# Weight products of a four-layer network: the outputs of a product take turns matmul by matmul, instead of one output after the other

## The reference, cut to what matters

```python
x = x + forgetting_attention(rmsnorm(x), fox_w_in, ..., fox_w_out)   # proj = h @ w_in ... o @ w_out
x = x + swiglu(rmsnorm(x), w_in, w_out)      # gu = h @ w_in; (silu(gate) * up) @ w_out, D_FF = 2816
x = x + retention(rmsnorm(x), w_in, w_out)   # w_in is 1024 x 6144, w_out 2048 x 1024
x = x + swiglu(rmsnorm(x), w_in, w_out)
x = x + rmsnorm_2(nsa_mixer(rmsnorm_2(x), ...))
x = x + rmsnorm_2(diff_mixer(rmsnorm_2(x), ...))
```

## Time and profile before

| | |
|---|---|
| median of 3 runs | 2217.71 us (2216.29 to 2219.92) |
| the profiled execution | 2220.15 us |
| its span | 2218.8 us |
| mean granted TensorE clock | 0.987 of full speed |
| PE busy | 2133.1 us, 96% of the span |
| DVE / ACT / POOL busy | 1002.5 / 783.7 / 254.8 us |
| DMA | 190.47 MB, 86 GB/s |

### The profile page before, as it was taken

How to read it: one execution, slowest core, us unless ns; L and a number is a source line. 1 busy time by engine, 2 the same in 40 slices (tenths; PEclk the granted TensorE clock), 3 DMA queues, 4 the chain that set the end, 5 groups by cost and what they waited for, 6 DMA issues and landing times.

```text
span 2218.8 us, 26618 instructions
## 1 busy us (share of the span) xinstructions
PE 2133.1 (96%) x10149; PEld 1720.7 (78%) x10149; DVE 1002.5 (45%) x2026; ACT 783.7 (35%) x1485; POOL 254.8 (11%) x360
## 2 busy tenths in 40 slices
PE   6999999999999999999999999899989999899978
PEld 4887887888878875888888888677867778688657
DVE  4437524444354336355434433543355553522575
ACT  4326332222232223333322222333355553332472
POOL 0103000000002100000100000010035552000250
PEclk9999999999999999999999999999999999999999
DMA  4330232333324320322333332243210002333211
GB/s 158 105 95 11 76 117 86 96 95 95 95 96 122 97 86 19 95 95 67 124 95 99 100 95 86 83 146 100 78 62 34 34 34 95 100 98 99 77 39 48
DMA packets 96766, 190.47 MB, mean 86 GB/s; under 512 B 8407, under 2 KB 16639, under 8 KB 96512
## 3 DMA queue, kind: packets, MB, share of 16 engines
q1 hardware_dynamic: 90288, 164.35, 24.6%
q0 software_dynamic: 6352, 24.41, 3.3%
HBM read 184.48 MB, written 4.26 MB: 85 GB/s over the span
## 4 chain that ended last, share of the span: by engine, by line
PE 86%; DVE 7%; ACT 4%; issue 2%; POOL 1%; DMA 0%; ACTq 0%; DVEq 0%; SPq 0%; POOLq 0%
PE bank L671 64%; PE bank L704 7%; PE bank L1095 4%; PE bank L1065 2%; PE bank L1076 2%; PE bank L936 2%; DVE wl L1742 1%; ACT junk L1259 1%; PE bank L1066 1%; DVE hTl L1814 1%; DVE xn L1804 1%; PE bank L921 1%; PE bank L1006 1%; PE bank L740 1%; PE bank L1102 1%
## 5 line engine op out<-in xcount | busy, mean ns | idle before, releaser
L1742 DVE TENSOR_TENSOR wl<-raw,wh 128x1024 fp32r<-128x1024 f32 x306 | 376.2, 1234 | 833.3 <-ACT wh L1220 832.6
L1220 ACT ACTIVATE wh<-raw 128x1024 fp32r<-128x1024 f32 x306 | 320.9, 1053 | 899.4 <-PE bank L671 875.5
L671 PE MATMUL bank<-hTh,wh 128*128 128x512 f32 (+1 forms) x1328 | 517.4, 390 | 0.2 <-issue 0.2
L671 PE MATMUL bank<-hTl,wh 128*128 128x512 f32 (+1 forms) x1328 | 516.8, 389 | 0.0
L671 PE MATMUL bank<-hTh,wl 128*128 128x512 f32 (+1 forms) x1328 | 516.7, 389 | 0.0
L671 PEld LDWEIGHTS bank<-hTh,wh 128*128 128x128 f32 (+1 forms) x1328 | 248.0, 187 | 53.6 <-issue 0.3
L671 PEld LDWEIGHTS bank<-hTh,wl 128*128 128x128 f32 (+1 forms) x1328 | 248.0, 187 | 53.0
L671 PEld LDWEIGHTS bank<-hTl,wh 128*128 128x128 f32 (+1 forms) x1328 | 248.0, 187 | 53.0
L671 PE MATMUL bank<-wh,hTh 128*128 128x512 f32 x464 | 181.6, 391 | 1.2 <-DVE hTl L2442 1.1
L671 PE MATMUL bank<-wh,hTl 128*128 128x512 f32 x464 | 180.7, 389 | 0.0
L671 PE MATMUL bank<-wl,hTh 128*128 128x512 f32 x464 | 180.6, 389 | 0.0
(11 more groups left out here) (351 smaller groups left out, 2784.7 us busy)
## 6 DMA issues: line engine op xcount, KB each, us to landing
raw<-in_ffn_w_in SPq DMA_DIRECT2D x88, 512.0 KB, 3.6
raw<-in_ret_w_in SPq DMA_DIRECT2D x48, 512.0 KB, 3.8
raw<-in_ffn_w_out SPq DMA_DIRECT2D x44, 512.0 KB, 3.7
raw<-in_diff_w_in SPq DMA_DIRECT2D x32, 512.0 KB, 3.7
raw<-in_fox_w_in SPq DMA_DIRECT2D x24, 512.0 KB, 3.8
raw<-in_nsa_w_in SPq DMA_DIRECT2D x20, 512.0 KB, 3.6
raw<-in_ret_w_out SPq DMA_DIRECT2D x16, 512.0 KB, 3.7
bt<-bias_by_lag POOLq DMA_DIRECT2D x16, 448.0 KB, 3.9
```

Of the source, the lines that this page charges most:

```text
L671: i = pe.do.matmul(dst, x, y, start=first and k == 0 and q == 0, stop=stop)
L1220: act.do.activation(M.hl[n % HL_SLOTS][0][:, 0:m], M.raw[n % RAW_SLOTS][:, 0:m], ACT.Copy).then_inc(*T.up("act_hi", n))
L1742: dve.do.tensor_tensor(wl[:, 0:m], M.raw[n % RAW_SLOTS][:, 0:m], wh[:, 0:m].bitcast(F32), ALU.subtract).then_inc(*T.up("dve_lo", n))
```

## The change

In every chunk but a product's last, the loops run k, then q, then o: the three matmuls of a step are each issued for all outputs in turn, so that successive matmuls go to different banks. The wait for the activations of a step and an output stands before the first of its three matmuls, and the wait for the bank behind it, in the product's first step. In the last chunk the order is that of before. A product of one chunk is all last chunk.

```diff
-        for o in range(n_out):
-            b = banks[o]
-            if first:
-                pe_bank(pe, T, b)
-            pe_weights(pe, T, n)
-            for k in range(nk):
-                for name, key in ready(k0 + k, None if mode == "F" else o):
-                    pe.wait_ge(*T.at(name, key))
...
-                for q, (x, y) in enumerate(parts):
-                    stop = last and k == nk - 1 and q == 2
-                    done = k == nk - 1 and q == 2 and o == n_out - 1
-                    i = pe.do.matmul(dst, x, y, start=first and k == 0 and q == 0, stop=stop)
...
+        pe_weights(pe, T, n)
+        if last:
+            for o in range(n_out):
+                if first:
+                    pe_bank(pe, T, banks[o])
+                for k in range(nk):
+                    operands(k, o)
+                    for q in range(3):
+                        step(o, k, q)
+                pe.free[banks[o]] = freed(o)
+        else:
             for k in range(nk):
...
+                for q in range(3):
+                    for o in range(n_out):
+                        if q == 0:
+                            operands(k, o)
+                            if first and k == 0:
+                                pe_bank(pe, T, banks[o])
+                        step(o, k, q)
```

More of the change, by code:

```diff
@@ L651, in pe_product, with step @@
         first, last = k0 == 0, k0 + nk == rows
-        for o in range(n_out):
+        def step(o, k, q):
             b = banks[o]
-            if first:
-                pe_bank(pe, T, b)
-            pe_weights(pe, T, n)
-            for k in range(nk):
-                for name, key in ready(k0 + k, None if mode == "F" else o):
-                    pe.wait_ge(*T.at(name, key))
[L660 to L667, removed]
-                for q, (x, y) in enumerate(parts):
-                    stop = last and k == nk - 1 and q == 2
-                    done = k == nk - 1 and q == 2 and o == n_out - 1
-                    i = pe.do.matmul(dst, x, y, start=first and k == 0 and q == 0, stop=stop)
[L672 to L675, removed]
@@ new lines, in step @@
+            h, l = operand(k0 + k)
+            if mode == "F":
+                f1 = min(width, o * 128 + 128)
+                x, y = wh[:, k, o * 128:f1], wl[:, k, o * 128:f1]
+                dst, (x, y) = M.bank[b][0:f1 - o * 128, :], ((x, h), (x, l), (y, h))[q]
+            else:
+                cols = slice(o * 128, o * 128 + 128)
+                dst, (x, y) = M.bank[b][:, 0:width], ((h[:, cols], wh[:, k, :]), (h[:, cols], wl[:, k, :]), (l[:, cols], wh[:, k, :]))[q]
+            stop = last and k == nk - 1 and q == 2
@@ new lines, in step, with operands @@
+            done = k == nk - 1 and q == 2 and o == n_out - 1
+            i = pe.do.matmul(dst, x, y, start=first and k == 0 and q == 0, stop=stop)
+            if stop or done:
+                i.then_inc(*T.up("pe_product", *[(tag, o)] * stop, *[("chunk", n)] * done))
+        def operands(k, o):
+            for name, key in ready(k0 + k, None if mode == "F" else o):
+                pe.wait_ge(*T.at(name, key))
+        pe_weights(pe, T, n)
[8 more added lines that the diff above has]
+                pe.free[banks[o]] = freed(o)
+        else:
+            for k in range(nk):
+                for q in range(3):
[5 more added lines that the diff above has]
+                        step(o, k, q)
```

## The result

The changed kernel is slower: ratio 1.0053 to the kernel before, 95% interval 1.0033 to 1.0073. Its four runs have a median of 2231.82 us (2226.51, 2231.55, 2232.1, 2232.4), beside 2218.82 us for the kernel before. On the earlier median of 2217.71 us the ratio gives 2229.5 us; the median of the four itself lies 0.8 us above the range's upper end. The profiled execution is the fastest of the four: 2226.51 us, span 2225.2 us, granted clock 0.986. In the changed kernel the matmul of the products stands on L666 and not L671, and the lines behind are 17 higher (in the experiments one to a few more).

The account below looks back on a forecast made before the run. PE's stream of matmuls was taken to bound the kernel. Waits of 2.3, 1.1 and 2.7 us plus 2.3 us for the clock made 8.4 us, from 2217.71 to about 2226.0 us; range 2220.5 to 2231 us.

Parts of the forecast that it names:

- The distance between matmuls: In all reordered chunks: time from one matmul to the next stays the same, 0 us, bounds -1 to +3 us.
- a switch that saves: Rival, all reordered matmuls: alternating banks cuts the fixed 0.0133 us per matmul, down to 2169 us with all; chance 0.05.
- a switch that costs: Rival, all reordered matmuls: each takes 0.229 us when banks alternate, 2236 us in all; chance 0.03.
- The new waits: First chunks of "nsa sw", "ret out0 0", "post1 0": PE waits for banks or operands, +2.3, +1.1, +2.7 us; taken as 6.0.
- diff z0: Product getting the banks of "diff v1": no wait, with 0.05 us to spare; named first for a possible new wait.
- The clock: In "post1 0": idle stretches make the clock fall for about 6.8 us, +2.3 us, bounds 0 to 3.2 us.
- the pauses of "nsa sw": Pauses of about 0.8 and 1.1 us there: no clock fall, 0 us; a fall would cost 1.6 to 3.2 us.
- Nothing takes these up later: Behind the three waiting products: unbroken PE streams follow, so no later work absorbs the delays.
- The forecast case: Waits in three products and a clock fall in "post1 0" only: 8.4 us, about 2226.0 us; chance 0.55.
- the rival with two falls: Clock falls in "nsa sw" as well as in "post1 0": 2228 to 2231 us; chance 0.07.
- The middle of the forecast: Whole kernel: sum of the waits and the clock fall, 8.4 us slower, median about 2226.0 us.

Follow-up runs that it names:

- e4: Changed kernel, but the first chunk of "nsa sw", "ret out0 0" and "post1 0" in the old order; ratio 1.0000 to the kernel before.
- e2: Changed kernel, but the first chunk of every product in the old order too; ratio 1.0000 to the kernel before.
- e1: The changed kernel measured once more without an edit; ratio 1.0046 to the kernel before, median 2230.82 us.
- e3: Changed kernel, but only the first chunk of each product of several chunks in the new order; ratio 1.0046 to the kernel before.
- e5: Changed kernel, but the old order everywhere except in the first chunk of "nsa sw"; ratio 1.0026 to the kernel before.
- e7: Changed kernel, but the old order everywhere except in the first chunk of "ret out0 0"; ratio 1.0003 to the kernel before.
- e9: Kernel before, with matmuls of 384 columns into unread banks in five pauses of PE; ratio 0.9982 to it, 2215.12 us.

## Why the prediction was right, and where it was off

**The distance between matmuls** was taken as unchanged, with -1 to +3 us as bounds. Right: 0.2267 us in the trace, and under 2 us in all by e4, in either direction. The argument that carried it was that a switch of banks was already in the old trace. The difference to the 215.8 ns, by a formula that the Trainium skill (TensorE: Matmul & The Clock Gate, Back-to-back issue gap) gives for an isolated matmul, is thus still there with a new bank at each matmul, so it is not about banks. The rivals on both sides of this, a switch that saves and a switch that costs, are out by e2 and e4. What the Trainium skill says of cycling through banks (TensorE: Matmul & The Clock Gate, A second HAM failure mode: psum-queue depth-cycling) doesn't describe this kernel either: 4248 matmuls cycle in e4 at the time of before.

**The new waits** were predicted in three products and nowhere else: 2.3, 1.1 and 2.7 us. The trace has 2.34, 1.08 and, at "post1 0", 4.83 us together with the clock. In the forecast's own reckoning, 0.31 us from the fourth matmul to the fifth and 20 at 0.2267 us, the second chunk would have begun at 2173.39 + 0.31 + 4.53 = 2178.23 instead of 2180.54. So 2.3 us are the clock's, as forecast, and 2.5 the waits', 0.2 less than forecast. "diff z0" stayed free of a wait: its second matmul came 0.34 us after the first, and the product took what it took before. That the other 73 products together cost under 2 us is shown by e4.

**The clock** was taken to fall in "post1 0", at a price of 2.3 us. It fell in all four traces with the new order there, for at least 6.6 us each time. The term that was mis-sized is the one for the pauses of "nsa sw": "there I take 0, with 1.6 to 3.2 us as the price of a fall". It falls there in two of four traces, at 1.6 us. That adds 0.8 us on average and brings the sum to 9.2 us. A second term was put at nothing: "Nothing takes these up later" looks only for what shortens a delay, and three of the four traces lost 1.95 to 2.1 us more in the layers behind "nsa sw", and it is open how much of that the change caused. The changed kernel was measured at 11.8 and 10.2 us with intervals of 7.3 to 16.2 and 7.5 to 13.1, which hold 9.2 and the predicted 8.4. The forecast case (fall in "post1 0" alone) is the profiled execution; the rival with two falls is e1. I gave the second 0.07, and it is the trace of two of the three kernels with all three waits (the changed kernel, e1, e3). In the times of these three, three executions, the profiled one among them, took 2224.9 to 2226.5 us and eleven 2230.0 to 2232.6. That the profiled execution agrees with the forecast so well is thus partly luck: it is one of the rarer, faster ones.

**Range and scatter.** The first four runs' median was 0.8 us above the range, the repeated measurement's 0.2 us below its end. Part of this is the reference: the kernel before was at 2217.71 us in three runs and at 2220.1 us or more in the larger sets. The middle of the forecast, 8.4 us, was short by 1.8 and 3.4 us of the two measurements, inside both intervals.

**What stays open** is whether "nsa sw" costs more than 3.9 us. e5 was timed at 5.8 us, and in its trace the layers behind "nsa sw" took 1.95 us longer than in the trace of before, with a low clock in other places. Whether this belongs to the delay or is scatter, as the 1.3 us in e7 seem to be, was not separated. Nor is it shown by an experiment that the pauses of "nsa sw" are what lets the clock fall there; e9 shows it for the older pauses.

## What to carry to other kernels

Before loops are interchanged so that outputs take turns, write down for each product when each bank is released and when each operand is ready: the first round through the outputs now wants them all within three matmuls. The steady state may be interchanged freely where a switch already costs nothing, as here, but the first chunk should keep the order in which the banks come free, as the last one must keep the order in which outputs are wanted. A short wait is priced at its length and, if it stands among little work, at the low clock behind it; filling the pause with matmuls that nobody reads cost nothing here and gained 4.0 us at the older pauses.

## What the runs showed of the hardware

- Writing a new bank at every matmul changes nothing that can be measured: 0.2267 us per matmul of 512 columns either way, and under 0.0005 us of difference by the times of e4.
- Pauses of 0.88 and 0.97 us with one matmul between them were followed by a granted clock of 0.50 in two of four traces. The pause of 1.55 us at "post1 0" was in four of four: in two of them the next matmul already ran at the low clock, in two the clock fell in the pause of 1.55 us behind it. The low stretches lasted over 3.2 us at "nsa sw" and over 6.6 us at "post1 0".
- Which of the older pauses lets the clock fall differs between executions of one program: at "gate00" it fell in the profiled changed kernel and not in e1, which is the same program, and cost 1.5 us. With these pauses filled, the eleven times of e9 spread over 3.4 us, those of the kernel before beside it over 8.7 us (21 times). How much of a kernel's spread they make was not measured further.
